# Projections for ssd and mlstm interleaved with rwkv's stages, their convolution read from PSUM, and their results stored elsewhere

## The chip, the cores and the metric

The kernel runs on one core of a Trainium2 chip. The metric is the device time of one execution in microseconds. The five engines run their own instruction streams in order and meet at semaphores: TensorE (PE), VectorE (DVE), ScalarE (ACT), GpSimd (POOL) and SyncE (SP), whose queue issues the loads of the weights.

## The reference, cut to what matters

Two networks follow each other on 256 tokens of width 1024. The change lies in the first, a block that is run for two layers:

```python
for l in range(DEPTH):                                   # DEPTH = 2
    x = x + FFN_HALF * swiglu(rms_norm(x, ffn1_norm[l]), ffn1_w_gate_up[l], ffn1_w_down[l])
    u = rms_norm(x, mix_norm[l]) @ w_in[l]
    u_ssd, u_ml, u_rw = jnp.split(u, [D_SSD_IN, D_SSD_IN + D_MLSTM_IN], axis=-1)
    y_ssd = ssd_mixer(u_ssd, ...)     # z, xbc, dt = split(u); xbc = silu(conv4(xbc)); state space scan
    y_ml = mlstm_mixer(u_ml, ...)     # xm, o, gates = split(u); xc = silu(conv4(xm)); q, k of xc, v of xm
    y_rw = rwkv7_mixer(u_rw, ...)     # token shift; decay, a, g by small products; delta-rule scan
    y = jnp.concatenate([y_ssd, y_ml, y_rw], axis=-1)
    x = x + y @ w_out[l]
    x = x + FFN_HALF * swiglu(rms_norm(x, ffn2_norm[l]), ffn2_w_gate_up[l], ffn2_w_down[l])
```

conv4 is a causal convolution over time with four taps a channel. ssd and mlstm need nothing of rwkv; all three need only u.

## The kernel before

Each stage is a class with one generator per engine (tensor, scalar, vector, gpsimd). The function network writes down one order of stages, phase by phase (run), and every engine walks through that order; within an engine work is done strictly in it. A stage's phases may alternate with another's in this order. Waits are semaphores (mark and wait_ge); enter waits for the ends of other stages.

Weights come in tiles of 1 MB (128 x 2048 floats). fetch, on SP, loads each into a raw place; the number of places that a stage may use is places. plan chooses a place and puts two operations for each tile into the order: split_hi (line 299, ScalarE) rounds the tile to the shorter float that TensorE multiplies faster, in one of two or three hi buffers, and split_lo (line 305, VectorE) writes what is left over the raw tile. They stand where the tile before it comes into use; split_hi waits for the landing and for the release of its buffer. mm3 multiplies with three matmuls (hi by hi, hi by lo, lo by hi), all issued from line 100.

For a layer, mixers puts these stages one behind another (ps0 to ps7 are the eight PSUM banks):

- ProjRw: seven tiles of w_in, rwkv's columns, banks 0 to 3; token shift into us.
- Prep: products for the norm of k (ss), the decay (w) and a (a), then rk; VectorE's chain with a reciprocal (L1133), the scan of the decay, and products; ScalarE's sigmoids and exponentials; eight groups of transposes (turns, L1078), copied by ScalarE and VectorE in turn (L1118, L1170).
- Inv: two masks T of 128 tokens; in each, eight products masked by VectorE (L1289, L1290), five levels of a triangular inversion (products x, ScalarE's copy X, products u, VectorE's updates L1308 and L1310), then bv, nT, nTT and the chunk products. Phases: 14.
- Scan: one phase. The state over chunks (S), then SA, then Y (128 recorded matmuls of 64 columns), then mean and variance by VectorE, a square by ScalarE (L1411), a power by GpSimd (L1419), and the last transposes and gate products, over which VectorE ends rwkv's result.
- ProjRest: 14 phases of a tile each, the columns of ssd and mlstm. Seven tiles give 14 channel blocks, which ScalarE copies from banks 0 to 3 to uT (L1511) and VectorE convolves (L1554, L1558) into xc; then ScalarE's silus (L1525). Six tiles of 512 columns give z and o (banks 4 to 7), one of 24 columns the gates (dg). It waits for all of Scan; it uses five raw places.
- Ssd and Mlstm, alternating phases, both after ProjRest; then Out with w_out, five raw places; then the next feed-forward stage.

uT, xc, zt, ot and dg lie over the memory that rwkv's stages use.

Of the kernel before, what the change touches and what calls it, by code (L numbers as in the profile page):

```python
# [151 lines left out]
class Core:  # L152


    def __init__(self, nc, A, ctx):
# [5 lines left out]
        self.raw = [Map(nc, at[i]).take(f"raw{i}", 2048) for i in range(RAW)]  # L161
        self.lo = [Map(nc, at[i]).take(f"lo{i}", 2048, dt=F32R) for i in range(RAW)]
# [56 lines left out]
    def plan(self):  # L219
# [4 lines left out]
        for pos, name in enumerate(self.order):  # L224
# [5 lines left out]
            for src, width in s.tiles.get(ph, ()):  # L230
# [4 lines left out]
                i = min(range(places), key=lambda i: turn.get(i, -1))  # L235
# [104 lines left out]
class Stage:  # L340
# [5 lines left out]
    phases, his, places, since, tail, spare, his_first = 1, 0, 0, (), 1, None, 0  # L346
# [581 lines left out]
class Mixer:  # L928


    def __init__(self, K, l):
# [3 lines left out]
        self.small = m.take(who + "small", 2560)  # L935
        self.sw = self.small[:, 0:1536].rearrange("p (w h e) -> p w h e", w=3, h=4)
        second = m.over(who + "ssd")
# [5 lines left out]
        self.ys = out.split("ys", 16, 256)  # L943
        rwkv = m.over(who + "rwkv")
# [17 lines left out]
        rest = m.over(who + "rest")  # L962
        self.uT, self.xc = rest.take("uT", 14, 259), rest.take("xc", 14, 256)
        self.zt, self.ot, self.dg = rest.take("zt", 2, 1024), rest.take("ot", 2, 512), rest.take("dg", 2, 24)
# [4 lines left out]
        self.Xt, self.xd = rest.take("Xt", 2, 1024), second.take("xd", 2, 1024)  # L969
        self.yy = second.take("yy", 2, 1024)  # L970
        self.sm = Loads(K.sem(f"small{l}"), 6)
# [14 lines left out]
class ProjRw(Stage):  # L986
# [18 lines left out]
    def load(self, a):  # L1005

        A, l, small = self.K.A, self.l, self.M.small
        for i, nm in enumerate(("mlstm_wq", "mlstm_wk", "mlstm_wv")):
            a().dma_start(self.M.sw[:, i], A[nm][l].rearrange("h d e -> d h e")).then_inc(*self.M.sm.mark())
        a().dma_start(small[0:64, 1536:2048], A["rwkv_w_up"][l]).then_inc(*self.M.sm.mark())  # L1010
        a().dma_start(small[64:128, 1536:2048], A["rwkv_a_up"][l]).then_inc(*self.M.sm.mark())
        a().dma_start(small[:, 2048:2560], A["rwkv_g_up"][l]).then_inc(*self.M.sm.mark())
# [30 lines left out]
class Prep(Stage):  # L1043


    def __init__(self, K, l, M, proj):
# [4 lines left out]
        self.turns = [lambda c, T: M.KR[:, 2 * c + T, 0, :], lambda c, T: M.ab[:, c, T * 128:T * 128 + 128],  # L1051
                      lambda c, T: self.k[:, c, T * 128:T * 128 + 128], lambda c, T: self.v[:, c, T * 128:T * 128 + 128]]

    def tensor(self, p):
        K, M, ps = self.K, self.M, self.K.ps
        t1 = M.t[1]
# [403 lines left out]
class ProjRest(Stage):  # L1460
# [14 lines left out]
    def tensor(self, p):  # L1475
        K, M, ps, hx = self.K, self.M, self.K.ps, self.M.hx
        self.enter(p)
        for q in range(7):
            if q >= 4:
                p.wait_ge(*self.ac["u", q - 4])  # L1480
# [1441 lines left out]
```

## Time and profile before

| | us |
|---|---|
| median of 3 runs | 3852.02 |
| lowest, highest | 3848.94, 3855.32 |
| the profiled execution | 3852.71 |
| its span, first to last instruction | 3850.9 |
| PE busy (share of the span) | 3411.2 (89%) |
| DVE busy | 2144.6 (56%) |
| ACT busy | 1301.1 (34%) |

The profile is of one execution. Busy time is the time in which an engine had an instruction under way. PEclk is the clock granted to TensorE as a share of 2.4 GHz: 0.50 is 1.2 GHz. In a timeline, what stands in brackets is how long the engine stood idle before the line and what ended that. One mm with plain floats is recorded as two matmuls. Both layers run the same stages: rwkv's stand at 283 to 490 us and at 1229 to 1432.

### The profile page before, as it was taken

The numbers are of one execution on the slowest core, as the hardware profiler recorded it, in microseconds if no ns is written. First come the engines' busy times: TensorE is split into PE (matmuls) and PEld (weight loads), VectorE is DVE, ScalarE is ACT, GpSimd is POOL, SyncE is SP. The second block draws the span as 40 slices with busy tenths as digits, with TensorE's granted clock in tenths as the row PEclk, the third lists the DMA queues.
The fourth block names the chain that finished last, engine by engine and source line by source line (L and its number), as shares of the span: only waits on it lengthen the run. The fifth ranks groups of instructions, "written<-read, shape, count | busy, mean of one in ns | idle before, by whom it ended". The sixth has DMA issues, their size and how long they took to land.

```text
span 3850.9 us, 46514 instructions
## 1 busy us (share of the span) xinstructions
PE 3411.2 (89%) x19298; PEld 2923.0 (76%) x19298; DVE 2144.6 (56%) x2625; ACT 1301.1 (34%) x1549; POOL 111.3 (3%) x114
## 2 busy tenths in 40 slices
PE   8986786699997778589899999999989998999899
PEld 7876676598986667579678786787878787777697
DVE  6746364577775635567675664584443333443454
ACT  4442133444434114244332223321232222343343
POOL 0001200000000210000000000000000000000000
PEclk9997787899998878789999999999999999999899
DMA  6540030355553003045534441243322222222352
GB/s 256 230 145 1 1 122 23 127 210 222 208 198 133 1 12 132 1 169 220 208 124 145 143 146 55 77 169 110 110 82 88 93 88 82 95 86 91 118 184 107
DMA packets 83654, 462.93 MB, mean 120 GB/s; under 512 B 7666, under 2 KB 11506, under 8 KB 43379
## 3 DMA queue, kind: packets, MB, share of 16 engines
q1 hardware_dynamic: 77664, 451.44, 32.0%
q10 hardware_dynamic: 5778, 8.52, 0.7%
q8 instruction: 152, 2.49, 0.3%
q14 instruction: 60, 0.48, 0.0%
HBM read 458.88 MB, written 1.05 MB: 119 GB/s over the span
## 4 chain that ended last, share of the span: by engine, by line
PE 63%; DVE 25%; ACT 8%; issue 2%; POOL 1%; ACTq 0%; DMA 0%; DVEq 0%; POOLq 0%
PE ps L100 62%; DVE lo L305 8%; DVE acc L449 5%; ACT hi L299 3%; DVE acc L446 0%; DVE xt L680 0%; PE ps L536 0%; PE ps L1078 0%; DVE m0restxc L1558 0%; DVE m1restxc L1558 0%; POOL st L611 0%; ACT rv L2501 0%; DVE f10rot L851 0%; DVE f20rot L851 0%; DVE f11rot L851 0%
## 5 line engine op out<-in xcount | busy, mean ns | idle before, releaser
L305 DVE TENSOR_TENSOR lo<-raw,hi 128x2048 fp32r<-128x2048 f32 (+1 forms) x357 | 808.1, 2264 | 718.1 <-ACT hi L299 697.9
L299 ACT ACTIVATE hi<-raw 128x2048 fp32r<-128x2048 f32 (+1 forms) x357 | 676.2, 1894 | 606.5 <-PE ps L100 577.6
L449 DVE SCALAR_TENSOR_TENSOR acc<-raw,sil,acc 128x512 f32<-128x512 f32 x504 | 379.0, 752 | 20.4
L100 PE MATMUL ps<-half00hs,hi 128*128 128x512 f32 x672 | 213.5, 399 | 4.3 <-DVE half00fin L678 4.3
L100 PE MATMUL ps<-half02hs,hi 128*128 128x512 f32 x672 | 212.5, 397 | 4.3 <-DVE half02fin L678 4.3
L100 PE MATMUL ps<-half10hs,hi 128*128 128x512 f32 x672 | 212.3, 397 | 4.3 <-DVE half10fin L678 4.3
L100 PEld LDWEIGHTS ps<-half10hs,hi 128*128 128x128 f32 x672 | 126.7, 189 | 34.5 <-issue 4.7
L100 PEld LDWEIGHTS ps<-half00hs,hi 128*128 128x128 f32 x672 | 126.8, 190 | 33.7 <-issue 4.7
L100 PEld LDWEIGHTS ps<-half02hs,hi 128*128 128x128 f32 x672 | 126.5, 189 | 33.8 <-issue 4.7
L100 PE MATMUL ps<-half00hs,lo 128*128 128x512 f32 x352 | 139.8, 397 | 0.0
L100 PE MATMUL ps<-half10hs,lo 128*128 128x512 f32 x352 | 139.5, 396 | 0.0
L100 PE MATMUL ps<-half02hs,lo 128*128 128x512 f32 x352 | 139.5, 396 | 0.0
L100 PE MATMUL ps<-half12hs,hi 128*128 128x256 f32 x704 | 127.2, 284 | 0.8 <-DVE half12hs L604 0.8
L100 PE MATMUL ps<-hi,half00hf 128*128 128x512 f32 x352 | 112.2, 399 | 1.8 <-DVE mods L459 1.4
L100 PE MATMUL ps<-hi,half02hf 128*128 128x512 f32 x352 | 110.8, 394 | 0.5 <-DVE lo L305 0.5
L100 PE MATMUL ps<-hi,half10hf 128*128 128x512 f32 x352 | 110.6, 394 | 0.0
L100 PE MATMUL ps<-f10hs_h,hi 128*128 128x256 f32 x352 | 102.1, 290 | 8.6 <-DVE lo L305 5.7
L100 PEld LDWEIGHTS ps<-half12hs,hi 128*128 128x128 f32 x704 | 108.4, 189 | 1.4 <-DVE half12hs L604 1.2
L100 PE MATMUL ps<-f21hs_h,hi 128*128 128x256 f32 x352 | 101.1, 287 | 4.4 <-DVE lo L305 3.6
L100 PE MATMUL ps<-f20hs_h,hi 128*128 128x256 f32 x352 | 101.1, 287 | 4.3 <-DVE lo L305 3.8
L100 PE MATMUL ps<-f11hs_h,hi 128*128 128x256 f32 x352 | 101.1, 287 | 2.6 <-DVE lo L305 2.2
L100 PE MATMUL ps<-f10hs_l,hi 128*128 128x256 f32 x352 | 100.1, 284 | 0.0
(912 smaller groups left out, 8223.2 us busy)
## 6 DMA issues: line engine op xcount, KB each, us to landing
raw<-in_ffn_w_gate_up SPq DMA_DIRECT2D x88, 1024.0 KB, 9.0
raw<-in_ffn_gu SPq DMA_DIRECT2D x88, 1024.0 KB, 4.8
raw<-in_ffn_w_down SPq DMA_DIRECT2D x85, 1024.0 KB, 5.6
raw<-in_ada_w SPq DMA_DIRECT2D x72, 1024.0 KB, 4.9
raw<-in_w_in_t SPq DMA_DIRECT2D x28, 1024.0 KB, 5.0
raw<-in_ret_w_in SPq DMA_DIRECT2D x24, 1024.0 KB, 4.9
raw<-in_w_out SPq DMA_DIRECT2D x16, 1024.0 KB, 4.9
raw<-in_w_in_n SPq DMA_DIRECT2D x12, 1024.0 KB, 5.0
```

Source lines behind the costliest of these rows:

```text
L100: return p().matmul(o, l, r, start=start, stop=stop, skip_group_check=True)
L299: a().activation(self.high(w), self.raw[self.place(r)][:, 0:width], ACT.Copy).then_inc(*a.mark(self.wac, w))
L305: v().tensor_tensor(self.low(w), self.raw[self.place(r)][:, 0:width], self.high(w).bitcast(F32), ALU.subtract).then_inc(*v.mark(self.wdv, w))
L449: v().scalar_tensor_tensor(out=acc[:, n, :], in0=w[:, k, :], scalar=s, in1=acc[:, n, :], op0=ALU.mult, op1=ALU.add).then_inc(*v.mark(self. ...
```

## The change

ProjRest is replaced by two stages. Rest does the same products in 112 phases of three or six matmuls in banks 4 to 7; RestOut takes the results from the banks in 19 phases: VectorE convolves ten of the 14 blocks straight from the bank (the last tap is now applied first, and the others are added shifted), ScalarE copies four blocks and the gates, and does the silus and sigmoids. Prep, Inv and Scan are cut into 6, 26 and 5 phases and use banks 0 to 3 only; in Prep the decay's products come ahead of the norm's, and the norm and the reciprocal after the scan of the decay. A hand-written order runs Rest's phases and RestOut's between rwkv's. Homes: xc and dg lie in raw places 3 and 4, so Rest has three raw places, and Out's tiles beyond the first three wait for the ends of Ssd and Mlstm if their place is 3 or above; zt, ot, Xt and mlstm's three small weights lie in rwkv's memory that is free by then, and these weights are loaded at the start of Scan instead of in ProjRw. Ssd and Mlstm wait for Scan and RestOut.

```diff
self.weights.append((s, n, len(self.tiles), width, pos))
-                i = min(range(places), key=lambda i: turn.get(i, -1))
+                i = min(range(s.near if n < s.near < 5 else places), key=lambda i: turn.get(i, -1))
                 count[i] += 1
...
         for src, width, s, _, i, _, before in self.tiles:
-            if i >= 5:
+            if i >= s.near:
                 s.enter(sp, s.since)
             if before is not None:
                 sp.wait_ge(*self.released(*self.tiles[before][2:4]))
...
+        far = Map(K.nc, K.far)
+        self.xc, self.dg = far.take(who + "xc", 14, 256), far.take(who + "dg", 2, 24)
+        assert far.at <= K.far + 2 * 8192
...
+    phases = 6
...
-        p.wait_ge(*self.ac["sq"])
-        for c in range(4):
-            mm(p, ps[c // 2][:, half(c)], K.bones, t1[:, c, :]).then_inc(*p.mark(self.pe, "ss", c))
+        yield
         p.wait_ge(*M.sm.all)
+        p.wait_ge(*A["tanh"])
         for j, name in enumerate(("w", "a")):
             rows = slice(64 * j, 64 * j + 64)
             for c in range(4):
-                cs = slice(1536 + c * 128, 1664 + c * 128)
-                mm(p, ps[2 + 2 * j + c // 2][:, half(c)], M.small[rows, cs],
+                mm(p, ps[2 * j + c // 2][:, half(c)], M.small[rows, c * 128:(c + 1) * 128],
                    M.us[rows, 12, :]).then_inc(*p.mark(self.pe, name, c))
+        p.wait_ge(*A["sq"])
+        p.wait_ge(*A["w", 3])
+        for c in range(4):
+            mm(p, ps[c // 2][:, half(c)], K.bones, t1[:, c, :]).then_inc(*p.mark(self.pe, "ss", c))
+        yield
+        p.wait_ge(*A["a", 3])
         p.wait_ge(*self.dv["rk", 3])
         for c in range(4):
-            mm(p, ps[6 + c // 2][:, half(c)], K.bones, t1[:, c, :]).then_inc(*p.mark(self.pe, "rk", c))
-        p.wait_ge(*self.dv["k"])
-        for q, src in enumerate(self.turns):
+            mm(p, ps[2 + c // 2][:, half(c)], K.bones, M.t[3][:, c, :]).then_inc(*p.mark(self.pe, "rk", c))
+        yield
+        p.wait_ge(*A["norm", 1])
...
-        M = self.M
+        M, l = self.M, self.l
         self.enter(a)
+        for i, nm in enumerate(("mlstm_wq", "mlstm_wk", "mlstm_wv")):
+            a().dma_start(M.sw[:, i], self.K.A[nm][l].rearrange("h d e -> d h e")).then_inc(*M.sl.mark())
+        for _ in range(4):
+            yield
         a.wait_ge(*self.dv["Yc"])
...
+class Rest(Stage):
+    his, phases, places = 2, 112, 3
+    def __init__(self, K, l, M, norm, prep):
+        super().__init__(K, "rest", f"rest{l}")
+        self.M, self.norm, self.prep = M, norm, prep
         for q in range(7):
+            self.tiles[8 * q] = [(K.A["w_in_t"][l, 7 + q], 2048)]
+        self.tiles[56] = [(K.A["w_in_s"][l], 192)]
         for q in range(6):
+            self.tiles[64 + 8 * q] = [(K.A["w_in_n"][l, q // 2, q % 2], 2048)]
+    def bank(self, q):
+        return self.K.ps[4 + q % 4]
     def tensor(self, p):
+        K, M, E, hx = self.K, self.M, self.pe, self.M.hx
         for q in range(7):
+            wh, wl = (w.rearrange("p (k n) -> p k n", k=8) for w in self.ready(p, q))
             if q >= 4:
+                p.wait_ge(*self.ev.dv["conv", 2 * q - 7])
+            for m in range(2):
+                c = slice(m * 128, (m + 1) * 128)
+                for k in range(8):
+                    self.norm.ready(p, k)
+                    x = mm3(p, self.bank(q)[:, m * 256:(m + 1) * 256], wh[:, k, c], wl[:, k, c], hx[0][:, k, :],
+                            hx[1][:, k, :], k == 0, k == 7)
+                    if (m, k) == (1, 7):
+                        x.then_inc(*p.mark(E, "tile", q))
+                    if k % 2:
+                        yield
...
         for q in range(3):
+            p.wait_ge(*(self.ev.ac["n", 0, 1] if q == 2 else self.ev.dv["conv", 13 if q else 11]))
+            p.wait_ge(*self.ev.ac["dg"])
             for kh in range(2):
+                n = 8 + 2 * q + kh
+                wh, wl = (w.rearrange("p (k n) -> p k n", k=4) for w in self.ready(p, n))
                 for T in range(2):
                     c = slice(T * 128, (T + 1) * 128)
                     for k in range(4):
                         kk = 4 * kh + k
+                        x = mm3(p, self.bank(2 * q + T)[:, :], hx[0][:, kk, c], hx[1][:, kk, c], wh[:, k, :], wl[:, k, :],
+                                kk == 0, kk == 7)
+                        if (T, k) == (1, 3):
+                            x.then_inc(*p.mark(E, "tile", n))
+                        yield
+class RestOut(Stage):
+    phases = 19
...
     def scalar(self, a):
+        K, M, E = self.K, self.M, self.rest.pe
+        for c in range(14):
+            if c in (10, 12):
+                a.wait_ge(*E["tile", c // 2])
+                a().activation(M.xm[:, c - 10:c - 8, :], v256(self.rest.bank(c // 2)),
+                               ACT.Copy).then_inc(*a.mark(self.ac, "xm", c))
+            yield
+        a.wait_ge(*E["tile", 7])
+        a().activation(M.dg, self.rest.bank(7)[:, 0:64].rearrange("p (t n) -> p t n", t=2)[:, :, 0:24],
+                       ACT.Copy).then_inc(*a.mark(self.ac, "dg"))
+        yield
+        for c in range(14):
+            a.wait_ge(*self.dv["conv", c])
+            a().activation(M.xc[:, c, :], M.xc[:, c, :], ACT.Silu, bias=K.col(self.l, "cb", c)).then_inc(*a.mark(self.ac, "xc", c))
+        yield
+        self.enter(a, [self.inv])
         for q in range(3):
+            a.wait_ge(*E["tile", 9 + 2 * q])
             for T in range(2):
+                o = M.zt[:, T, q * 512:(q + 1) * 512] if q < 2 else M.ot[:, T, :]
+                a().activation(o, self.rest.bank(2 * q + T)[:, :],
+                               ACT.Silu if q < 2 else ACT.Sigmoid).then_inc(*a.mark(self.ac, "n", q, T))
+            yield
     def vector(self, v):
+        K, M, D = self.K, self.M, self.dv
+        for c in range(14):
+            q = c // 2
+            if c < 10:
+                v.wait_ge(*self.rest.pe["tile", q])
+                u = self.rest.bank(q)[:, half(c)]
+            else:
+                v.wait_ge(*self.ac["xm", c - c % 2])
+                u = M.xm[:, c - 10, :]
+            v().tensor_scalar(M.xc[:, c, :], u, K.col(self.l, "cw", 4 * c + 3), None,
+                              ALU.mult).then_inc(*v.mark(D, "tap", c, 0))
+            for s in range(1, 4):
+                key = ("conv", c) if s == 3 else ("tap", c, s)
+                v().scalar_tensor_tensor(out=M.xc[:, c, s:256], in0=u[:, 0:256 - s], scalar=K.col(self.l, "cw", 4 * c + 3 - s),
+                                         in1=M.xc[:, c, s:256], op0=ALU.mult, op1=ALU.add).then_inc(*v.mark(D, *key))
+            yield
+        for _ in range(5):
+            yield
...
-        rest = put(f"rest{l}", ProjRest(K, l, M, norm, [scan]))
-        ssd, ml = put(f"ssd{l}", Ssd(K, l, M, rest)), put(f"ml{l}", Mlstm(K, l, M, rest))
+        rest = put(f"rest{l}", Rest(K, l, M, norm, prep))
+        ev = put(f"rout{l}", RestOut(K, l, M, rest, inv))
+        ssd, ml = put(f"ssd{l}", Ssd(K, l, M, scan, ev)), put(f"ml{l}", Mlstm(K, l, M, scan, ev))
         ssd.ml = ml
         out = put(f"out{l}", Out(K, f"out{l}", [ssd, ml], A["w_out"][l], M.yT, M.ys, Whole(K.xa), 5))
+        out.near, out.since = 3, [ssd, ml]
+
+        def beside(s, *counts):
+
+            for n in counts:
+                run(s)
+                for i in range(n):
+                    run(rest)
+
+        def conv(n=1):
+            for _ in range(n):
+                run(ev)
+
         join(before, norm)
-        for s in (prw, prep, inv, scan, rest):
-            for _ in range(s.phases):
-                run(s)
+        for _ in range(prw.phases):
+            run(prw)
+        beside(prep, 4, 14, 6, 4, 4, 0)
+        conv(2)
+        for T in range(2):
+            beside(inv, 2)
+            for i in range(5):
+                beside(inv, 1)
+                conv()
+                beside(inv, 1 if T or i > 2 else 2)
+            conv()
+            beside(inv, 1, 1 + T)
+        conv(2)
+        beside(scan, 6, 6, 8, 16)
+        conv()
+        beside(scan, 12)
+        conv(2)
         for s in "smsmsmsmsmsmmsmsmmsmsmmsmsmmsmsmmsmsmmsm":
```

## Rows read from the trace of the kernel before

**Rows 1.** page: span; by slices of 96 us, granted clock and bytes moved

```profile
span 3850.9 us, 46514 instructions
...
PEclk9997787899998878789999999999999999999899
...
GB/s 256 230 145 1 1 122 23 127 210 222 208 198 133 1 12 132 1 169 220 208 124 145 143 146 55 77 169 110 110 82 88 93 88 82 95 86 91 118 184 107
```

**Rows 2.** layer 0: stretch, us, busy (count) of PE, PEld, DVE, ACT, POOL, clock, DMA share

```profile
283.00:326.00 43.00, 19.28 (x66) 15.16 (x66) 32.93 (x37) 18.85 (x26) 0.00 (x0) 0.56 0.05 21
326.00:382.00 56.00, 46.89 (x416) 43.22 (x416) 27.81 (x47) 7.76 (x13) 16.52 (x12) 0.91 0.00 1
382.00:437.80 55.80, 45.76 (x368) 42.58 (x368) 28.56 (x49) 7.76 (x13) 16.60 (x12) 0.87 0.00 1
437.80:447.40 9.60, 7.69 (x96) 7.15 (x96) 3.07 (x6) 0.00 (x0) 0.00 (x0) 0.50 0.01 2
447.40:470.80 23.40, 23.32 (x128) 19.49 (x128) 0.69 (x1) 0.00 (x0) 0.00 (x0) 0.50 0.00 1
470.80:481.30 10.50, 0.00 (x0) 0.00 (x0) 5.76 (x6) 2.97 (x2) 3.11 (x2) 0.50 0.00 0
481.30:489.70 8.40, 4.33 (x17) 3.44 (x17) 5.07 (x9) 0.00 (x0) 0.00 (x0) 0.70 0.00 0
489.70:587.00 97.30, 86.04 (x528) 77.80 (x528) 55.46 (x71) 40.82 (x42) 0.00 (x0) 0.90 0.39 131
587.00:704.50 117.50, 60.01 (x342) 53.94 (x341) 62.62 (x133) 36.55 (x82) 6.87 (x6) 0.73 0.03 10
```

**Rows 3.** the same view: ProjRest of layer 1

```profile
1431.60:1529.00 97.40, 85.75 (x528) 77.37 (x528) 55.44 (x71) 41.14 (x44) 0.00 (x0) 0.90 0.39 131
```

**Rows 4.** timeline, prep and the first mask of inv: start, us, engine, line

```profile
292.14 0.69 DVE L1132 TENSOR_SCALAR m0rwkvprept<-m0rwkvprept 128x1024 f32<-128x1024 f32 x1 [6.95 <-ACT m0rwkvprept L1098]
292.86 6.55 DVE L1133 RECIPROCAL m0rwkvprept<-m0rwkvprept 128x1024 f32<-128x1024 f32 x1
...
327.21 0.42 DVE L1289 TENSOR_TENSOR m0yT<-ps,mask 128x256 f32<-128x256 f32 x1 [1.38 <-PE ps L100]
```

**Rows 5.** instruction groups by form within ProjRest: busy us, mean ns, idle before

```profile
L305 DVE TENSOR_TENSOR lo<-raw,hi 128x2048 fp32r<-128x2048 f32 x13 | 29.8, 2293 | 37.6 <-ACT hi L299 37.2
L299 ACT ACTIVATE hi<-raw 128x2048 fp32r<-128x2048 f32 x12 | 23.0, 1916 | 6.8 <-PE ps L100 5.9
L1558 DVE SCALAR_TENSOR_TENSOR m0restxc<-m0restuT,cols,m0restxc 128x256 f32<-128x256 f32 x42 | 20.4, 485 | 1.5
...
L1525 ACT ACTIVATE m0restxc<-m0restxc,cols 128x256 f32<-128x256 f32 x14 | 7.1, 508 | 3.7 <-DVE m0restxc L1558 3.2
L1554 DVE TENSOR_SCALAR m0restxc<-m0restuT,cols 128x256 f32<-128x256 f32 x14 | 5.0, 354 | 1.3 <-DVE lo L305 0.5
...
L1519 ACT ACT_TABLE_LOAD x1 | 1.3, 1283 | 0.1
```

**Rows 6.** one line's instructions, min/median/max ns: a 256-column operation from a bank

```profile
L589 DVE TENSOR_SCALAR mn0no<-ps,cols x4: 483/484/484, 229.6 to 233.5; 128x256 f32<-128x256 f32 x4
```

**Rows 7.** timeline, TensorE in inv: its waits at the first and a later level

```profile
336.76 1.25 PE L100 MATMUL ps<-m0rwkvTm,m0rwkvCT 128*128 128x128 f32 x8 [2.52 <-DVE m0rwkvTm L1295]
...
356.38 1.13 PE L100 MATMUL ps<-m0rwkvTm,m0rwkvCT 128*128 128x128 f32 x8 [0.66 <-DVE m0rwkvTT L1310]
```

**Rows 8.** busy time by stretch: 256-column matmuls of the projections at full clock

```profile
500.00:530.00 30.00, 30.00 (x253) 30.00 (x252) 21.18 (x26) 13.25 (x11) 0.00 (x0) 1.00 0.57 194
```

**Rows 9.** timeline: 512-column matmuls at full clock

```profile
577.17 0.39 PE L100 MATMUL ps<-hi,m0hx_h 128*128 128x512 f32 x1
577.40 0.39 PE L100 MATMUL ps<-lo,m0hx_h 128*128 128x512 f32 x1
```

**Rows 10.** busy time by stretch: the end of the 24-column matmuls

```profile
583.50:586.90 3.40, 3.40 (x17) 3.40 (x17) 2.21 (x1) 0.00 (x0) 0.00 (x0) 0.50 0.27 111
```

**Rows 11.** DMA issues: KB each, median us to landing

```profile
raw<-in_w_in_t SPq DMA_DIRECT2D x28, 1024.0 KB, 5.0
```

More of the change, by code:

```diff
@@ L340 @@
 class Stage:
-    phases, his, places, since, tail, spare, his_first = 1, 0, 0, (), 1, None, 0
+    phases, his, places, since, tail, spare, his_first, near = 1, 0, 0, (), 1, None, 0, 5
     def __init__(self, K, kind, who, after=()):
@@ L934, in __init__ @@
         self.l = l
-        self.small = m.take(who + "small", 2560)
-        self.sw = self.small[:, 0:1536].rearrange("p (w h e) -> p w h e", w=3, h=4)
-        second = m.over(who + "ssd")
+        self.small, self.xm = m.take(who + "small", 1024), m.take(who + "xm", 4, 256)
+        m.at = K.free + 10240
         self.hx = m.split(who + "hx", 8, 256)
@@ L1095, in scalar @@
         a().activation(t1, t0, ACT.Square).then_inc(*a.mark(self.ac, "sq"))
+        yield
+        for c in range(4):
+            a.wait_ge(*self.pe["w", c | 1])
+            a().activation(M.sgw[:, c, :], ps[c // 2][:, half(c)], ACT.Sigmoid,
+                           bias=K.col(l, "w0", c)).then_inc(*a.mark(self.ac, "w", c))
+        for c in range(4):
+            a.wait_ge(*self.pe["a", c | 1])
+            a().activation(M.ab[:, c, :], ps[2 + c // 2][:, half(c)], ACT.Sigmoid,
+                           bias=K.col(l, "a0", c)).then_inc(*a.mark(self.ac, "a", c))
         a.wait_ge(*self.pe["ss", 3])
@@ L1114, in scalar @@
         a().activation(M.cwb, M.cwb, ACT.Exp, scale=-DECAY).then_inc(*a.mark(self.ac, "fall"))
-        for n in range(0, 8, 2):
-            o, i = self.turned(n)
-            a.wait_ge(*self.pe["turn", n])
-            a().activation(o, i, ACT.Copy).then_inc(*a.mark(self.ac, "turn", n))
+        yield
+        self.turn_act(a, 0)
+        self.turn_act(a, 2)
+        yield
+        self.turn_act(a, 4)
+        yield
+        self.turn_act(a, 6)
         yield
@@ L1171, in vector @@
+        yield
+        self.turn_dve(v, 7)
         yield
 class Inv(Stage):
-    phases = 14
+    phases = 26
     def __init__(self, K, l, M, prep):
@@ L1270, in scalar @@
                 yield
+                yield
             for q in range(2):
@@ L1348, in gpsimd @@
                 yield
+                yield
+            yield
             yield
 class Scan(Stage):
+    phases = 5
     def __init__(self, K, l, M, inv):
@@ L1416, in gpsimd @@
         self.enter(g)
+        for _ in range(4):
+            yield
         g.wait_ge(*self.dv["va"])
@@ L1459, in vector @@
         yield
-class ProjRest(Stage):
-    his, phases, places = 2, 14, 5
-    def __init__(self, K, l, M, norm, after):
-        super().__init__(K, "prest", f"prest{l}", after)
-        self.l, self.M, self.norm = l, M, norm
+class Rest(Stage):
[3 more added lines that the diff above has]
+        self.M, self.norm, self.prep = M, norm, prep
         for q in range(7):
-            self.tiles[q] = [(K.A["w_in_t"][l, 7 + q], 2048)]
+            self.tiles[8 * q] = [(K.A["w_in_t"][l, 7 + q], 2048)]
+        self.tiles[56] = [(K.A["w_in_s"][l], 192)]
@@ new lines, in tensor @@
+        wh, wl = (w.rearrange("p (k n) -> p k n", k=8) for w in self.ready(p, 7))
+        p.wait_ge(*self.ev.dv["conv", 7])
+        for T in range(2):
+            c = slice(T * 128, (T + 1) * 128)
+            for k in range(8):
+                x = mm3(p, self.bank(7)[:, T * 32:T * 32 + 24], hx[0][:, k, c], hx[1][:, k, c], wh[:, k, :], wl[:, k, :],
+                        k == 0, k == 7)
+                if (T, k) == (1, 7):
+                    x.then_inc(*p.mark(E, "tile", 7))
+                if k % 2:
+                    yield
```

232 lines of the change are left out of this document (98 added, 134 removed).

## The prediction

> **What bounds the kernel now.** I read the slices of the page first. DMA moves 1 GB/s in four slices: twice a stretch of about 200 us in which hardly any weight is loaded, and in the same slices the granted clock sags [rows 1]. These are rwkv's stages of the two layers. Then the busy time by stretch of layer 0 [rows 2]: prep is 283 to 326, inv 326 to 437.8, scan 437.8 to 489.7, ProjRest 489.7 to 587, ssd and mlstm to 704.5. From 283 to 489.7 TensorE stands still for 23.7 + 9.1 + 10.0 + 1.9 + 0.1 + 10.5 + 4.1 = 59.4 us, and much of what it does runs at half clock (0.56 in prep, 0.50 from 437.8 to 481.3). Then ProjRest occupies it alone for 97.3 us, and for 97.4 in layer 1 [rows 2, 3]. So the bound changes: in prep it is VectorE's chain, which waits 6.95 us for the norm and then spends 6.55 on a reciprocal [rows 4]; in inv it is TensorE with 0.66 us of waiting a level [rows 7]; in scan it is TensorE at half clock, then a chain DVE, ACT, POOL, DVE; in ProjRest it is TensorE.
>
> **What moves.** ProjRest's products: 336 of 256 columns, 48 of 24, 144 of 512. At full clock 253 take 30.0 us, 0.119 each [rows 8]; 512 columns take 0.23 [rows 9]; I price the 24-column ones as the 256-column ones. 384 x 0.119 + 144 x 0.23 = 78.8 us. They become 112 phases of 0.7 us: 32 beside prep, 32 beside inv, 48 beside scan. The stage of 97.3 us is gone; what counts is how much longer the other stages get. The floor: 59.4 us of idle time, plus half of the work at or near half clock (9 of 19.3 us in prep, 3.8 of 7.7 and 11.7 of 23.3 in scan: 24.5), against 78.8 of work: by TensorE alone rwkv would get no longer at all (-5 us). The split operations and the convolution move with them: 13 lo splits of 2.29 us on VectorE, 13 hi splits of 1.92 on ScalarE, 14 convolutions of 3 x 0.485 + 0.354 = 1.8, some 1.95 with gaps [rows 5]. VectorE is in order, so each of them stands in rwkv's chain.
>
> **Prep: +10.8 us.** VectorE has 32.9 us of work in 43 [rows 2]. Added ahead of inv's first mask: four lo splits (9.2) and two convolutions (3.9), together 46.0. Its long wait for the norm goes, since the decay matmuls come first and the reciprocal last; what is left is the wait for the first sigmoids, about 4.8 us, because ScalarE now does a hi split (1.92) before them. New is a wait for the hi split of rest tile 3: its buffer is free only when tile 1 is through on TensorE, some 14 phases late, about 3.5 us; behind it on ScalarE stand the exponentials, on VectorE the norm and the reciprocal. 46.0 + 8.3 = 54.3 from 283.7 gives 338.0 for inv's first mask, against 327.2 [rows 4]. Bounds: +6 if the splits fit the waits that are there, +15 if TensorE's phases run at half clock.
>
> **Inv: +10.5 us.** 32 phases are 22.7 us. They find 19.1 us idle [rows 2], but only where they are put: per mask 1.4 of the 2.52 before the first level, 0.7 within it, 0.66 at each of five level borders [rows 7], 5.5 in all, 11 for both. The clock is 0.91 and 0.87, some 10 us of half clock a mask; I count 4 us back in all. Against that a lo split (2.29) and a convolution (1.95) in the same level make VectorE late by about 3. 22.7 - 11 - 4 + 3 = 10.7. Bounds +4 and +17.
>
> **Scan: +17 us.** Before 51.9 [rows 2]. New, from its start: 8 phases and two small steps, 7.1; then rest tile 9 is not split yet, since ScalarE has the 14 silus to do (7.1 busy [rows 5], about 7.5 with gaps), a table load of 1.28 [rows 5], three DMA issues that this change puts there, and the hi split; ready at about 11.5. Four phases, the SA step, 8 phases: 23 at full clock, 27 at half. Then Y, 23.4 at half clock [rows 2], 11.7 at full. Behind Y the chain took 10.5 us. Now ScalarE has ahead of its square a hi split that waits for 12 phases (8.3 + 1.9), then the two silus of z with a table load (2.5); square, sum, POOL's power, product as before: 19.7. Then 12.5 for the last step and 12 phases, over VectorE's tail. 23 + 11.7 + 19.7 + 12.5 = 67, and I take 69 with part of the start at half clock: +17. With Y at half clock 82, +30. Below, +7 if the last hi split is no wait. **Why Y at full clock:** before, it starts at half clock and stays there though TensorE is busy 23.32 of 23.40 us [rows 2]; in the new order eight dense phases stand right before it, and it need only hold what they reach. The nearest row speaks against: 24-column matmuls that began at full clock behind 512-column ones end at 0.50, busy all the time [rows 10]. Y's have 64 columns, so I take the full clock, at six chances in ten, and the rest as a case.
>
> By the Trainium skill (TensorE: Matmul & The Clock Gate, Part 1, What's actually happening) the default is the throttled clock and busy time releases it. The trace disagrees in Y, busy throughout and never released. If busy time alone were enough the old Y would have been warm and this step would give nothing, which is why I keep its 11.7 us as a case of its own.
>
> **Smaller terms.** ssd waits for ProjRest's successor, whose last act is a table load and two sigmoids (2.5) where it was the gates' copy (0.8): +2, as ssd's own chain starts from there. Ten of the convolutions read a bank instead of SBUF: a plain 256-column operation from a bank takes 0.483 against 0.354 [rows 5, 6], 10 x 0.13 = 1.3 us of VectorE, beside inv's matmuls, where VectorE is busy half the time: nothing, 1.3 without that cover. Seven copies of 0.6 on ScalarE become two: nothing, ScalarE is not late there. The three small DMAs leave ScalarE's queue in the first projection, at most -1.5. SP's queue: rest has three raw places instead of five; a tile lands 5.0 us after issue [rows 11] and a place is refilled while two tiles of 5.7 us are used, so nothing; bound in the rivals. Two of w_out's tiles now wait for the end of ssd and mlstm; they land within 10 us, and their turn comes after three tiles of over 5 us each: nothing, 5 if not.
>
> By the skill (ScalarE: Activation LUTs, What ACT_TABLE_LOAD costs) a switch costs a load of 1.28 us and a drain of about 1.38. The row has the load and 0.1 us of idle time before it [rows 5], and no drain. By the page the three loads that I put on the path would be 4.1 us dearer a layer, and the time 8 us longer.
>
> **Sum.** A layer: 10.8 + 10.5 + 17 + 2 = 40.3 longer, 97.3 gone, 57 saved; 114 for two. The profiled execution took 3852.7 (span 3850.9 [rows 1]), 0.7 over the median of the runs: 3852.7 - 114 = 3738.7, say 3738.5 us.
>
> **Rivals.**
> *Nearly all fits* (0.20). The splits fall into waits: prep +6, inv +4, scan +7, ssd +1: 79 saved a layer, 3694. For it: the floor by TensorE is below zero, and ScalarE is busy a fifth of rwkv's time. Against: VectorE and ScalarE are in order, and the splits stand ahead of chain steps.
> *Y stays at half clock and splits come late* (0.20). 14 + 15 + 30 + 2 = 61 longer, 37 saved a layer, 3779. For it: the 24-column row, and Y's own.
> *Slower: tiles come one at a time* (0.05). With three raw and two hi places each tile could be fetched only when the one before is through; then landing, hi and lo, 5.0 + 1.92 + 2.29 = 9.2 us, stand in rwkv's chain for each of 13 tiles: 120 a layer against 97.3, 3898. It decides from 7.5 us a tile. Against: four slices with 1 GB/s leave the queues empty, and the tile after next is always on its way.
> *The stages do not interleave* (0.03). If every phase waits for the step before it through a semaphore, the work is only laid out otherwise: 3853.
>
> **Chances.** The forecast has 0.52, its own range 3714 to 3764 (prep, inv and scan each off by some 5 us a layer). For 8 in 10 the range must take in most of the two neighbours: 3690 to 3785. A measurement of this kernel can tell 0.2%, 7.7 us, from no change. Faster 0.92, same 0.03, slower 0.05.
>
> **What would show it.** In the profile after: no stretch of dense projections between rwkv and ssd; inv's first mask 11 us later after the first projection's end; the reciprocal after the decay scan, with a wait for ACT's hi split before it; inv's levels longer by their two or three phases less the 0.66 us that TensorE waited; Y's 128 matmuls in about 12 us at clock 1.0; POOL's power some 20 us behind Y. The forecast is wrong if Y shows 0.50, if TensorE waits for lo splits in most tiles, or if inv's levels wait for VectorE by more than 3 us.

## The result and the profile after

The changed kernel takes 3787.99 us (median of 4 runs, 3785.44 to 3789.53) against 3850.55 (4 runs beside it): ratio 0.9835, 95% interval 0.9818 to 0.9852. It is faster by 63 us where 114 were forecast, and just above the range (3785). The profiled execution has a span of 3787.5 us, 63.4 less than before.

The page after, span, granted clock and GB/s in slices of 95 us. The four slices with 1 GB/s [rows 1] are down to one:

```profile
span 3787.5 us, 46520 instructions
...
PEclk9998977899999887799899999999999999999899
...
GB/s 254 221 136 46 34 76 1 174 216 222 209 214 106 24 54 45 53 213 223 151 178 117 167 123 40 109 155 123 91 78 89 95 89 73 106 78 100 118 187 102
```

Busy time by stretch of layer 0 after, in the columns of [rows 2]: prep, inv's two masks, scan until Y, Y in two parts, Y's end to the last step, the last step until ssd, ssd and mlstm:

```profile
282.70:336.00 53.30, 39.09 (x272) 36.51 (x272) 45.45 (x47) 27.15 (x30) 0.00 (x0) 0.90 0.23 79
336.00:405.90 69.90, 59.33 (x512) 56.06 (x514) 45.59 (x74) 10.05 (x15) 18.49 (x12) 0.90 0.05 18
405.90:469.50 63.60, 55.66 (x452) 51.81 (x449) 42.91 (x71) 11.08 (x17) 18.41 (x12) 0.91 0.05 17
469.50:498.30 28.80, 23.32 (x157) 18.66 (x158) 8.82 (x11) 14.14 (x18) 0.00 (x0) 0.78 0.37 116
498.30:503.10 4.80, 4.80 (x46) 4.01 (x45) 1.69 (x1) 0.00 (x0) 0.00 (x0) 0.98 0.31 130
503.10:518.20 15.10, 15.10 (x86) 12.63 (x85) 0.74 (x2) 0.00 (x0) 0.00 (x0) 0.50 0.01 1
518.20:539.50 21.30, 15.45 (x49) 11.39 (x49) 10.29 (x8) 6.08 (x5) 3.11 (x2) 0.80 0.29 98
539.50:555.30 15.80, 12.85 (x52) 10.23 (x52) 7.23 (x9) 7.09 (x8) 0.00 (x0) 0.89 0.31 98
555.30:675.50 120.20, 65.66 (x341) 58.69 (x342) 61.03 (x133) 34.73 (x78) 6.85 (x6) 0.69 0.02 8
```

By the first VectorE operation of each stage (k's first product, the first mask, scan's memset, ssd's dt):

| layer 0, us | before | after | |
|---|---|---|---|
| prep | 43.5 | 53.4 | +9.9 |
| inv | 109.9 | 133.4 | +23.5 |
| scan, ProjRest, until ssd | 152.4 | 86.0 | -66.4 |
| of this, ProjRest | 97.3 | none | scan +31 |

That is -33.0 in layer 0. In layer 1 the same marks give +9.8, +26.3 (inv took 107.2 there before) and -65.5, so -29.4; the spans give -63.4 in all. ssd and mlstm are 4.9 us longer (120.2 against 115.3 by the same marks) with the same waits at a lower clock (0.69 against 0.73), and from there to layer 1's first mask, with prep's 9.9 taken off, it is 5.7 shorter (562.1 against 567.8), so the two cancel. w_out's tiles in three places cost nothing: TensorE's longest wait from its first product on is 7.4 us in both traces, for the same VectorE operation.

Prep came as forecast, inv and scan did not. By the same marks, inv before (the two masks together; after, they are the second and third line above, 115.0 us busy of 133.5):

```profile
327.20:437.10 109.90, 91.45 (x776) 84.62 (x773) 55.80 (x93) 15.53 (x26) 33.12 (x24) 0.89 0.00 1
```

TensorE is idle for 18.5 us before and after, although 32 phases were put in to fill such gaps. The group of its first product of a level, with its idle time before it, over both masks, before and after:

```profile
L100 PE MATMUL ps<-m0rwkvTm,m0rwkvCT 128*128 128x128 f32 x160 | 24.9, 305 | 10.7 <-DVE m0rwkvTm L1295 5.4 <-DVE m0rwkvTT L1310 5.3
L100 PE MATMUL ps<-m0rwkvTm,m0rwkvCT 128*128 128x128 f32 x160 | 25.1, 310 | 9.6 <-DVE m0rwkvTT L1355 8.2 <-DVE m0rwkvTm L1339 1.4
```

The waits for Tm, at each mask's first level, are mostly filled (5.4 to 1.4), and those for VectorE's differences in TT have grown instead (5.3 to 8.2). One level after, on VectorE and then on ScalarE (timeline: start, us, engine, line; the wait in brackets):

```profile
364.81 0.69 DVE L1353 TENSOR_TENSOR m0rwkvTm<-m0rwkvTm,ps 128x512 f32<-128x512 f32 x1 [3.31 <-PE ps L100]
...
367.32 0.69 DVE L1355 TENSOR_TENSOR m0rwkvTT<-m0rwkvTT,ps 128x512 f32<-128x512 f32 x1
372.45 2.29 DVE L306 TENSOR_TENSOR lo<-raw,hi 128x2048 fp32r<-128x2048 f32 x1 [4.45 <-ACT hi L300]
374.85 0.48 DVE L1631 TENSOR_SCALAR m0xc<-ps,cols 128x256 f32<-128x256 f32 x1
375.37 1.52 DVE L1635 SCALAR_TENSOR_TENSOR m0xc<-ps,cols,m0xc 128x255 f32<-128x255 f32 x3
377.00 0.69 DVE L1353 TENSOR_TENSOR m0rwkvTm<-m0rwkvTm,ps 128x512 f32<-128x512 f32 x1
```

```profile
369.80 0.60 ACT L1311 ACTIVATE m0rwkvX<-ps 128x512 f32<-128x512 f32 x1 [0.30 <-PE ps L100]
370.51 1.91 ACT L300 ACTIVATE hi<-raw 128x2048 fp32r<-128x2048 f32 x1
```

VectorE is done with a level at 368.0, waits 4.45 us for ScalarE's hi split (which stands behind the copies of the same level), makes the lo split and a convolution, and comes to the next level's difference at 377.00: 12.2 us between two levels. The product that it subtracts had been ready, since no wait stands in brackets there. It is the only one of the three large lo splits in inv (350.70, 372.45, 440.45) with such a wait.

### The profile page after: what moved, and what is told of

Same layout as the page of the kernel before. It is cut to its first block, busy times and chain, and to the rows that moved or that the text cites. A ratio compares the mean times of both kernels' runs of the same rounds, so it can differ in the third digit from the quotient of the medians.

```text
span 3787.5 us, 46520 instructions
## 1 busy us (share of the span) xinstructions
PE 3405.8 (90%) x19298; PEld 2914.4 (77%) x19298; DVE 2150.8 (57%) x2623; ACT 1292.3 (34%) x1535; POOL 118.9 (3%) x114
## 4 chain that ended last, share of the span: by engine, by line
PE 63%; DVE 25%; ACT 8%; issue 2%; POOL 1%; ACTq 0%; DMA 0%; DVEq 0%; POOLq 0%
PE ps L100 62%; DVE lo L306 8%; DVE acc L450 5%; ACT hi L300 3%; PE ps L537 0%; DVE acc L447 0%; DVE xt L681 0%; DVE m1xc L1635 0%; DVE m0xc L1635 0%; POOL st L612 0%; ACT rv L2581 0%; DVE f20rot L852 0%; DVE f11rot L852 0%; DVE f10rot L852 0%; DVE f21rot L852 0%
## 5 line engine op out<-in xcount | busy, mean ns | idle before, releaser
L100 PE MATMUL ps<-f10hs_h,lo 128*128 128x256 f32 x352 | 100.4, 285 | 0.0
```

The source lines that it names most:

```text
L100: return p().matmul(o, l, r, start=start, stop=stop, skip_group_check=True)
```

## The experiments

All are the changed kernel with the edit shown. Each time is the median of four runs (ten for the block), each ratio is to the kernel before. Stage times are read by the marks of the table above, in layer 0. The first four try the large parts.

**The order alone put back.** Everything else of the change stays.

```diff
-        beside(prep, 4, 14, 6, 4, 4, 0)
...
-        conv(2)
+        for s, n in ((prep, 6), (inv, 26), (scan, 5)):
+            for _ in range(n):
+                run(s)
+        for q in range(7):
+            for _ in range(8):
+                run(rest)
+            conv(2)
+        for _ in range(8):
+            run(rest)
+        conv(2)
+        for n in (16, 16, 16):
+            for _ in range(n):
+                run(rest)
+            conv()
```

> The changed kernel with only the order put back: prep, inv and scan run alone, then the 112 phases, with the convolutions two by two behind their tiles. Prep's new order, the convolution from the banks, the three raw places and the new homes stay. Theory (the interleaving is the whole gain, the other edits cost and give nothing): prep, inv and scan take again about 43, 110 and 52 us, the dense stage 97, and the time is the one of before, 3851 within 8. Rival 1 (Prep's new order and the copies that are gone give something by themselves, the wait of 6.95 for the norm being gone): about 3840. Rival 2 (the other edits cost: ssd and mlstm are 5 us longer a layer in the changed kernel): about 3861.

3833.97 us, ratio 0.9948 (0.9933 to 0.9962): 21 us faster than before, so the first theory and rival 2 fall and rival 1 has the sign. Its stretches (prep, inv, scan, the dense stage):

```profile
279.10:319.60 40.50, 20.85 (x74) 16.34 (x76) 32.39 (x36) 17.55 (x25) 0.00 (x0) 0.60 0.00 0
319.60:427.80 108.20, 90.31 (x776) 84.06 (x773) 55.76 (x93) 15.52 (x26) 33.11 (x24) 0.89 0.00 1
427.80:479.40 51.60, 38.46 (x268) 33.52 (x269) 14.35 (x23) 2.96 (x2) 3.11 (x2) 0.54 0.06 16
479.40:576.20 96.80, 82.83 (x503) 72.78 (x501) 57.47 (x72) 39.51 (x40) 0.00 (x0) 0.93 0.40 138
```

Prep is 3.0 shorter than before, inv 1.7, and from scan's last operation to ssd's first 3.9 (96.8 against 100.7): 8.6 a layer from all the edits but the order. The new order in prep, the copies left out and the gates' place are the likely sources; they were not run apart. The interleaving itself is worth only 3834 - 3788 = 46 us (44 by the spans), some 23 a layer. Against this run prep got 12.9 longer, inv 25.2 and scan 34.4. In the dense stage of this run the phases that went beside prep take 23.3 us (until tile 4 begins at 502.7), those beside inv 26.2 (until tile 8 at 529.0) and the rest until ssd 47.3. So the 32 phases beside prep save 23.3 - 12.9 = 10.4, the 48 beside scan 47.3 - 34.4 = 12.9, and **the 32 beside inv 26.2 - 25.2 = 1.0**. Prep's 12.9 are four lo splits and two convolutions, 9.2 + 3.9 = 13.1: there VectorE is the bound and each of its operations counts in full.

**Inv's 32 phases in one block ahead of inv.**

```diff
+        for n in (0, 1, 1, 0, 1, 1, 1, 1):
+            for _ in range(4):
+                run(rest)
+            conv(n)
...
-                beside(inv, 1)
-                conv()
-                beside(inv, 1 if T or i > 2 else 2)
+                beside(inv, 0)
+                if i % 2 == 0:
+                    conv()
+                beside(inv, 0)
```

> The changed kernel with inv's 32 phases run in one block between prep and inv, with six of the convolutions; the other six stay in inv, one in every other level. Theory (in inv the interleaving hides nothing: the 32 phases are 22.7 us of work and inv got 23.6 us longer): the block takes 23 us, inv falls from 133.5 back to about 112, and the time stays within 8 of the changed kernel's 3788. Rival 1 (VectorE's splits and convolutions bound the block, four of 2.29 and six of 1.95, or it runs at half clock): the block takes 32 to 40, about 3810 to 3820. Rival 2 (inv without splits gets back more than it gave, since the late splits cost more than the work): 3775.

3847.44 us, ratio 0.9980 (0.9970 to 0.9989), worse than every theory. Inv falls to 110.1, as expected, but prep with the block takes 108.6 instead of 53.4. The block costs 55 us. TensorE's waits in it (timeline):

```profile
346.40 0.55 PE L100 MATMUL ps<-m0hx_h,hi 128*128 128x256 f32 x1 [6.54 <-DVE m0xc L1635]
359.02 0.55 PE L100 MATMUL ps<-m0hx_h,hi 128*128 128x256 f32 x1 [5.20 <-DVE m0xc L1635]
375.57 0.36 PE L100 MATMUL ps<-hi,m0hx_h 128*128 128x24 f32 x1 [8.68 <-DVE m0xc L1635]
```

It is a ring of waits: the convolution that frees a bank stands in VectorE's order behind the lo split of the tile after next, that waits for the hi split, and that for TensorE to be through with the tile before. My block was badly put together, so this run says nothing on how good a dense block can be. It does show that inv without phases and splits, but with three convolutions a mask, is back at 110.

**One tap of the convolution instead of four**; three taps are left out.

```diff
-            for s in range(1, 4):
-                key = ("conv", c) if s == 3 else ("tap", c, s)
-                v().scalar_tensor_tensor(out=M.xc[:, c, s:256], in0=u[:, 0:256 - s], scalar=K.col(self.l, "cw", 4 * c + 3 - s),
-                                         in1=M.xc[:, c, s:256], op0=ALU.mult, op1=ALU.add).then_inc(*v.mark(D, *key))
```

> The changed kernel with one of the four taps of the convolution; the other three (42 VectorE operations a layer, 1.45 us of each convolution) are left out. Theory 1 (inv is late because VectorE, in order, has a split and a convolution in one level): 12 convolutions lose 17.4 us of VectorE in inv, some 8 to 10 us of it on the path, and prep loses 2.9; the time falls by about 24, to 3764. Theory 2 (inv is longer by TensorE's own work, 22.7 us of phases, and VectorE is late only beside it): only prep gets shorter, about 3782.

3750.6 us, ratio 0.9733 (0.9719 to 0.9748). Inv falls by 15.6 us of the 17.4 that VectorE was relieved of, more than I had expected of theory 1. The TensorE work was untouched. Inv as a whole in this run:

```profile
330.10:447.90 117.80, 106.57 (x968) 98.86 (x965) 70.20 (x109) 21.98 (x34) 37.11 (x24) 1.00 0.06 21
```

TensorE's idle time is 11.2 us (18.5 in the changed kernel), and its busy time is 8.4 less, at clock 1.00 instead of 0.91. Here a late VectorE cost twice, by the wait and by the clock.

**All lo splits five steps later** in VectorE's order; ScalarE's hi splits stay.

```diff
-                split(e, w)
+                if name == "ac" or not self.behind(w):
+                    split(e, w)
+            for w in self.delayed.get(pos, ()) if name == "dv" else ():
+                split(e, w)
...
+                        self.delayed.setdefault(min(at + by, self.weights[w][4] - 1), []).append(w)
```

> The changed kernel with every lo split of the moved tiles put five steps later in VectorE's order, behind the next two steps of the stage that it stands in, at the latest right before the tile's first use; the hi splits stay. No wait for ScalarE's hi split (4.45 us in the level at 372 us, 3.79 in prep) then stands ahead of the chain's operations. Theory (those waits are on the path): prep and inv fall by about 3 and 4 us a layer, the time to about 3774. Rival (TensorE waits for the lo split instead, or the wait only moves to the next operation): 3788 within 5.

3790.51 us, ratio 0.9835 (0.9820 to 0.9849), no change; the trace shows why. Inv falls by 12.4 (to 121.0), but prep grows by 7.5, scan until Y's end by 1.3, and the end of the stage by 5.8. In prep TensorE now waits for the lo split itself (waits of TensorE in prep: us in total, times, longest):

```profile
PE ps L100 <- DVE lo L316: 17.1, 3, 6.6
```

So both readings were right, each in its place. That gave the next run.

**Lo splits later in inv alone** (`inv_span` holds the steps of the order in which inv stands).

```diff
-                    if self.behind(w):
+                    if self.weights[w][0].inv_span[0] <= at < self.weights[w][0].inv_span[1]:
```

> The changed kernel with the lo splits that stand in inv put five steps later in VectorE's order; those in prep and scan stay where they are. In the run where all of them were moved back, inv fell by 12.4 us (133.4 to 121.0), prep rose by 7.5 and the end of the stage by 5.4. Theory (in inv the wait of the lo split for ScalarE's hi split holds up the chain; in prep and at the end TensorE waits for the split itself): inv 121, prep 53, 12 us saved a layer, 3764. Rival (the time only moves from prep into inv, since the same splits must be made): inv 133, 3788.

3764.84 us, ratio 0.9778 (0.9764 to 0.9793), as expected to a microsecond. Inv, and the same lo split as above, which now stands one level later (VectorE; the first two lines begin the level where it stood before and the one where it stands now):

```profile
333.00:454.20 121.20, 108.85 (x960) 102.53 (x960) 88.51 (x146) 20.92 (x31) 36.08 (x24) 0.94 0.06 19
```

```profile
357.43 0.69 DVE L1372 TENSOR_TENSOR m0rwkvTm<-m0rwkvTm,ps 128x512 f32<-128x512 f32 x1
...
364.64 0.69 DVE L1372 TENSOR_TENSOR m0rwkvTm<-m0rwkvTm,ps 128x512 f32<-128x512 f32 x1 [2.14 <-PE ps L100]
...
367.15 0.69 DVE L1374 TENSOR_TENSOR m0rwkvTT<-m0rwkvTT,ps 128x512 f32<-128x512 f32 x1
367.94 2.29 DVE L317 TENSOR_TENSOR lo<-raw,hi 128x2048 fp32r<-128x2048 f32 x1
370.27 0.48 DVE L1650 TENSOR_SCALAR m0xc<-ps,cols 128x256 f32<-128x256 f32 x1
370.79 1.51 DVE L1654 SCALAR_TENSOR_TENSOR m0xc<-ps,cols,m0xc 128x255 f32<-128x255 f32 x3
372.41 0.69 DVE L1372 TENSOR_TENSOR m0rwkvTm<-m0rwkvTm,ps 128x512 f32<-128x512 f32 x1
```

VectorE's busy time in inv is the same to 0.01 us (88.51). The split waits for nothing now. The level that it left takes 7.2 us instead of 12.2, and the one where it stands 7.8 instead of 8.3.

So the level with the wait gives 5.0 of the 12.2 us by which inv gets shorter. Most of the rest lies at the two other large splits, which had no wait in brackets. There the split itself (3.17 and 3.16 us) stood ahead of the level's differences: the level of each gets 3.3 and 2.4 us shorter, the one behind it 1.0 and 0.7. The second mask's first level gets 1.4 longer. What the wait and what the place is worth was not run apart.

By TensorE's busy time, 6.1 of the 12.2 us are idle time (18.5 to 12.4) and 6.1 the clock (115.0 busy to 108.9). The loss in inv was the order, not the work, which is the same in both runs.

**Square first:** square, sum of squares and power directly behind Y, z's first silus ahead of Y.

```diff
-        for _ in range(4):
+        for _ in range(3):
             yield
         a.wait_ge(*self.dv["Yc"])
...
-        beside(scan, 6, 6, 8, 16)
+        beside(scan, 6, 6, 8)
         conv()
-        beside(scan, 12)
+        beside(scan, 16, 12)
```

> The changed kernel with ScalarE's square (and the sum of squares and POOL's power) right behind Y, and z's first silus ahead of Y in the order, so that neither the hi split that waits for 12 phases (25.93 us of waiting, until 523.60) nor the next one nor z's silus stand ahead of the square. Theory (my step on the end of scan: ScalarE's order makes it 21.3 us from Y's end to the last step where it was 10.5): the last step starts 12 us behind Y, 9 saved a layer, 3770. Rival (the 16 phases and their lo splits take that time anyway, VectorE and TensorE being the bound there): 3786.

3769.72 us, ratio 0.9793 (0.9779 to 0.9808). ScalarE behind Y, in the changed kernel and then in this run (its Y ended 1.7 us sooner):

```profile
523.60 1.92 ACT L300 ACTIVATE hi<-raw 128x2048 fp32r<-128x2048 f32 x1 [25.93 <-PE ps L100]
529.20 1.91 ACT L300 ACTIVATE hi<-raw 128x2048 fp32r<-128x2048 f32 x1 [3.68 <-PE ps L100]
531.14 1.23 ACT L1617 ACTIVATE m0zt<-ps 128x512 f32<-128x512 f32 x2
532.46 1.06 ACT L1469 ACTIVATE m0rwkvscanYb<-m0rwkvscanYc 128x1024 f32<-128x1024 f32 x1
```

```profile
519.90 1.06 ACT L1469 ACTIVATE m0rwkvscanYb<-m0rwkvscanYc 128x1024 f32<-128x1024 f32 x1 [23.06 <-DVE m0rwkvscanYc L1508]
521.50 1.92 ACT L300 ACTIVATE hi<-raw 128x2048 fp32r<-128x2048 f32 x1 [0.54 <-PE ps L100]
```

The square moves from 14.3 us behind Y to 3.4, and the hi split behind it still waits 0.54 for TensorE, so it lost nothing. From Y's end to ssd 6.7 us less.

**Silus beside Y** instead of at scan's start.

```diff
-        conv(2)
-        beside(scan, 6, 6, 8, 16)
+        conv()
+        beside(scan, 6, 6, 8)
+        conv()
+        beside(scan, 16)
```

> The changed kernel with the 14 silus of the convolution put behind the SA step in ScalarE's order, beside Y, instead of at scan's start. Theory (TensorE waits 4.69 us at 485 for a tile whose hi split stood behind the silus; VectorE waited 10.44): scan's start until Y falls from 28.7 to 24 us, 4.7 saved a layer, 3778. Rival (the silus then stand ahead of the hi splits behind Y and the square, and the time is given back there): 3788.

3769.92 us, ratio 0.9792 (0.9776 to 0.9809), twice the gain expected. Before Y, TensorE waited for a lo split in the changed kernel and does not in this run:

```profile
PE ps L100 <- DVE lo L306: 4.7, 1, 4.7
```

From scan's start to Y's first copy 30.2 us instead of 37.0. Of the 6.8 the wait is 4.7; where the rest comes from was not followed up. Behind Y nothing was given back (37.4 against 37.3 until ssd).

**Y in four pieces**, three phases of rest between each two.

```diff
-            x.then_inc(*p.mark(E, "Y", j))
-        yield
+                if T:
+                    x.then_inc(*p.mark(E, "Y", j))
+                yield
...
-        beside(scan, 6, 6, 8, 16)
+        beside(scan, 6, 6, 8, 3, 3, 3, 7)
```

> The changed kernel with Y in four pieces of four groups, three phases of rest between each two, seven behind the last (16 as before). Theory (Y falls to half clock 4.8 us after its start because its own matmuls do not hold the full clock, and dense phases of 512 columns in between do): the 16 groups take 13.6 us at 0.85 each instead of 19.9, and the square comes earlier since 9 of the 12 phases that it waits for are done; 6 to 12 saved a layer, 3764 to 3776. Rival (the clock falls all the same): Y's groups take 19 to 23 us, only the square's wait is gained and lost again before the last step, 3786.

3774.38 us, ratio 0.9798 (0.9779 to 0.9818). Y and the pieces of rest by turns (the last columns are clock, DMA share, GB/s):

```profile
495.40:498.70 3.30, 3.30 (x34) 2.76 (x32) 1.68 (x1) 0.00 (x0) 0.00 (x0) 1.00 0.43 181
498.70:500.90 2.20, 2.20 (x12) 1.80 (x11) 0.00 (x0) 0.00 (x0) 0.00 (x0) 1.00 0.00 0
500.90:504.20 3.30, 3.30 (x34) 2.76 (x32) 0.00 (x0) 0.00 (x0) 0.00 (x0) 1.00 0.00 0
504.20:506.40 2.20, 2.20 (x12) 1.81 (x11) 0.69 (x1) 1.20 (x1) 0.00 (x0) 1.00 0.28 34
506.40:509.70 3.30, 3.30 (x34) 2.76 (x32) 2.29 (x1) 0.71 (x1) 0.00 (x0) 1.00 0.74 300
509.70:513.30 3.60, 3.60 (x12) 2.77 (x11) 0.00 (x0) 0.00 (x0) 0.00 (x0) 0.56 0.00 0
513.30:516.70 3.40, 3.40 (x34) 2.86 (x32) 0.00 (x0) 0.00 (x0) 0.00 (x0) 0.97 0.00 0
```

The 16 groups take 13.3 us instead of 19.9. The clock falls once, to 0.56 for 3.6 us of rest's phases behind the third piece, and is back for the fourth. In layer 1 it does the same at the same place.

**All of them together.** Three edits (lo splits in inv, square first, silus and z beside Y), then with Y in four pieces, then with the convolutions that wait for ScalarE's copy one step behind it. The order of three edits:

```diff
-        conv(2)
-        beside(scan, 6, 6, 8, 16)
+        conv()
+        beside(scan, 6, 6, 8)
+        conv(2)
+        beside(scan, 16, 12)
```

With four, its last line is `beside(scan, 3, 3, 3, 7, 12)`; the fifth edit, in VectorE's program of the convolutions:

```diff
+            if c == 10:
+                yield
```

> The three edits together that were each run alone: lo splits of inv five steps later, square first, silus (and z's first ones) beside Y. By the traces of the single runs they gave, a layer, 12.2 us in inv, 6.7 behind Y and 6.8 ahead of Y. Theory (three separate places of the chain): they add, 25.7 a layer, 3736. Rival (silus, z and square all stand on ScalarE beside and behind Y and meet there: 8.3 + 1.2 of silus and two hi splits of 1.9 in the 20 us of Y): one of the two scan gains is lost, 3750.

3731.80 us, ratio 0.9695 (0.9679 to 0.9711). They add: 56 us less than the changed kernel, where the single traces sum to 51 and the single runs to 60.

> The same three edits with Y in four pieces and phases of rest in between. Theory (Y's groups at full clock: 14.9 us instead of 19.8 by the single run): 4.9 a layer less than the run with three edits, 3727. Rival (fewer phases are left behind Y, seven instead of 16, so TensorE stands still until the product of Y is there, and the clock falls for the last step and ssd): no change against three edits, 3737.

3727.84 us, ratio 0.9678 (0.9663 to 0.9692). From scan's start to ssd 69.7 us against 72.6. The step is 2.9 a layer by the trace and not 4.9. TensorE waits 3.9 us for the normed Y where it waited 2.9, so 1.0 of the missing 2.0 is the rival's reason; the runs' intervals overlap.

> The four edits, and the convolutions of blocks 10 to 13, which wait for ScalarE's copy of the bank, one step later in VectorE's order than that copy. Theory (the same fault as with the lo splits: VectorE waits in order for a ScalarE operation that was given out in the same step; 2.57 and 3.51 us in the second mask): 3 us a layer less than four edits, 3721. Rival (inv's levels are then bound by TensorE or by VectorE's work itself): no change, 3727.

3734.08 us, ratio 0.9694 (0.9679 to 0.9708): the theory falls, and against four edits the intervals overlap. Inv takes 123.2 and 121.3 us in the two layers, against 121.3 and 121.3. The wait for the copy is gone, but the level's first difference now waits 3.82 us for TensorE (at 429.44), and the last convolution stands ahead of scan's first operation. That a wait stands in brackets does not make it dear.

The version with four edits is 3.2% faster than the kernel before and 60 us faster than the changed one.

## Why the prediction was off, point by point

- **Prep, +10.8: right** (+9.9), and by its reason, VectorE's own sum: against the run with only the order put back the increase is the splits and convolutions to 0.2 us. Of the two waits in that sum the one for tile 3's hi split was 1.25 us and not 3.5; gaps between operations, which the sum left out, made up for it, and that is luck.
- **Inv, +10.5: mis-sized** (+23.5), and the largest fault. The sum was 22.7 of work, less 11 hidden, less 4 of clock, plus 3 for a late VectorE. Measured by the marks: idle time 18.5 before and after, so on balance nothing was hidden; TensorE's busy time rose from 91.5 to 115.0, the whole work and 0.8 more, so the clock gave nothing. The failed step is the term of 3 us for a late VectorE. Only the order of the lo splits was changed to take 12.2 us off again, so the term was some 15, and it ate up the hiding and the clock's share. I put a split and a convolution side by side as 2.29 + 1.95 and left out two things. The lo split stands in the same step as its hi split and can wait for it, with the level's differences queued behind (one level, which got 5.0 us shorter). And a split that waits for nothing, but stands ahead of the differences, delays them and what TensorE does with them (the other levels). I had seen the pair in ProjRest: 37.2 of VectorE's 37.6 us of idle time there is the wait for ScalarE [rows 5]. With the splits five steps later inv is +11.3, near the forecast, but made up otherwise: 6.1 hidden, and 17.4 more of busy time.
- **Scan, +17 and ssd +2: mis-sized** (+31 together). Forecast were +17 and +2. Two steps failed: the start took 28.8 instead of 23 (rest tile 9 was split 15.5 us after scan's start, where 11.5 was put; with the silus beside Y TensorE does not wait for it), and Y 19.9 instead of 11.7. From Y's end to the last step it was 21.3 where 19.7 was forecast, which is near. What comes behind it until ssd took 15.8, where 12.5 + 2 was put.
- **Y's clock: half right.** It began at full clock, as the dense phases before it were to give, and fell to 0.50 after 4.8 us, as the 24-column row had warned [rows 10]. I gave "it need only hold what they reach" six chances in ten against the only row that bore on it. The rival with Y at half clock (3779) had the nearest time, and its other half, splits that come late, is near what happened in inv. Nor is full clock half the time: Y's groups take 13.3 us at 0.97 to 1.00 against 23.4 at 0.50.
- **Other edits at nothing:** the banks as the convolution's source, the homes and the three raw places cost nothing that shows. But I credited the new order of prep and the copies left out only inside other terms; with the rest of the edits they give 8.6 us a layer. By the sum, 57 forecast, less 13.0 in inv, less 12 in scan, plus 1 in prep is 33, and 31.7 a layer was measured.
- **The slower rival** (tiles one at a time) did not come: TensorE's waits for lo splits in prep are 0.8 us. A relative of it, the ring through two hi places and a bank, is what made the block ahead of inv cost 55 us.

By the Trainium skill (TensorE: Matmul & The Clock Gate, Part 1, What's actually happening) the clock follows how busy TensorE has been recently. The rows of Y speak against it once more: busy 15.10 of 15.10 us at 0.50, right after 4.8 us at full clock.

## What to carry to other kernels

When work is woven into a latency chain, its order on each in-order engine counts more than its amount: an operation that waits for another engine, or is simply long, holds up everything queued behind it, so give it out where the chain has no operation due, and only where its own reader can spare the time. Moved back, the lo splits gained 12 us a layer in inv and lost 7.5 in prep, and the convolutions behind their copies gained nothing. Price a woven-in step as wait plus work on every queue that it passes, and look for the same pair of instructions elsewhere in the trace: a long wait there is a warning. Compare with a run in which only the order is put back before crediting the weaving.

## What the runs showed of the hardware

VectorE and GpSimd hold each other up when both read two operands from SBUF. A lo split takes 2.29 us alone, and 3.17 beside GpSimd products, of which the second takes 3.15 instead of 1.27; an operation with a bank as a source keeps its 0.69 beside one (timeline of the changed kernel):

```profile
350.70 3.17 DVE L306 TENSOR_TENSOR lo<-raw,hi 128x2048 fp32r<-128x2048 f32 x1
...
358.75 0.69 DVE L1355 TENSOR_TENSOR m0rwkvTT<-m0rwkvTT,ps 128x512 f32<-128x512 f32 x1
```

```profile
350.19 4.82 POOL L1392 TENSOR_TENSOR m0rwkvCT<-m0yT,msk 128x512 f32<-128x512 f32 x2
351.87 3.15 POOL L1392 TENSOR_TENSOR m0rwkvCT<-m0yT,msk 128x512 f32<-128x512 f32 x1
358.89 1.27 POOL L1392 TENSOR_TENSOR m0rwkvCT<-m0yT,msk 128x512 f32<-128x512 f32 x1 [3.88 <-PE ps L100]
```

The line of x2 holds both products; the second is shown by itself below it. It happens at two of the three large lo splits in inv. What it costs on the path was not measured. By the Trainium skill (Trainium Architecture — The Big Picture, What this means for kernel authors) the two engines share a port pair by an exclusive lock. The trace agrees: the split begins 0.5 us after the first product and is 0.88 us longer, and the second product ends 1.15 us after the split, about its own length.

TensorE's clock fell in the middle of matmuls of 64 columns that left no gap: to 0.50 after 4.8 us, and after 5.0 in layer 1. With pieces of 3.3 us of them and 2.2 us of 512-column matmuls in between it fell once in each layer, behind the third piece. Why it fell there is open.
